# Gated recurrence with the second half of its tokens in reversed order: one level product for chunk j and chunk j+4, three merged key buffers

## What is computed

```python
qf = silu(q) * DK ** -0.5
logf = minimum(log_sigmoid(z) + log1p(lb * exp(-z)), 0)   # z = clip(f, -30, 30)
kf = -expm1(logf)
# per head, over tokens t:  state = exp(logf_t) * state + outer(kf_t, v_t);  o_t = qf_t @ state
# in chunks: o = (qf * exp(bcum)) @ state_before
#              + sum over j <= i of (qf_i . exp(bcum_i - bcum_j) . kf_j) v_j
o = rmsnorm(o, norm_g) * silu(g)
```

## Time and profile before

| | us |
|---|---|
| median of 3 runs (lowest, highest) | 2679.35 (2674.05, 2681.57) |
| the profiled execution, its own time | 2681.49 |
| its span from first to last instruction | 2679.7 |
| PE busy | 2566.4 (96%) |
| DVE busy | 1528.2 (57%) |
| POOL busy | 1217.8 (45%) |
| ACT busy | 575.9 (21%) |
| PE products of L470 (896 records), busy | 104.7 |
| mean granted TensorE clock, share of full | 0.984 |

### The profile page before, as it was taken

The page is one execution under the profiler, slowest core; times in us unless marked ns, Lnnn a source line. Parts: engine busy times, 40 slices in busy tenths (PEclk is TensorE's granted clock), DMA queues, the critical chain, the costliest instruction groups (busy, mean ns, idle before and its releaser), DMA issues.

```text
span 2679.7 us, 32172 instructions
## 1 busy us (share of the span) xinstructions
PE 2566.4 (96%) x11898; PEld 2120.0 (79%) x11898; DVE 1528.2 (57%) x1639; ACT 575.9 (21%) x737; POOL 1217.8 (45%) x941
## 2 busy tenths in 40 slices
PE   8999999899999999999899999977989999999997
PEld 5788877788888888888778787766878888888885
DVE  6794666677777773976675747544572222531223
ACT  3110344322222222111121214233331100121000
POOL 0433332222222222333577677711766666766663
PEclk9999999999999999999999999989999999999998
DMA  6322111111111111433644344321433223432323
GB/s 227 118 71 90 63 59 63 55 38 42 39 39 39 39 47 69 151 118 110 237 167 161 126 141 158 129 83 43 154 114 98 94 95 101 151 101 94 102 95 110
DMA packets 84882, 269.87 MB, mean 101 GB/s; under 512 B 7888, under 2 KB 9296, under 8 KB 83792
## 3 DMA queue, kind: packets, MB, share of 16 engines
q1 hardware_dynamic: 71760, 243.80, 27.2%
q10 hardware_dynamic: 13056, 25.17, 2.7%
HBM read 224.37 MB, written 44.56 MB: 100 GB/s over the span
## 4 chain that ended last, share of the span: by engine, by line
PE 77%; DVE 12%; issue 4%; ACT 4%; DMA 2%; POOL 1%; DVEq 0%; SPq 0%; ACTq 0%; POOLq 0%
PE ps L349 22%; PE ps L350 22%; PE ps L351 22%; PE xb L470 4%; DVE macc L701 1%; DVE lxc L904 1%; PE ps L397 1%; POOL w_lo L1813 1%; DVE lgx L704 1%; DVE lga L926 1%; DMA w_kv<-wall 1%; DVE cdev L707 1%; DVE xb L837 1%; DVE xa L837 1%; DVE yb_lo L689 1%
## 5 line engine op out<-in xcount | busy, mean ns | idle before, releaser
L1813 POOL TENSOR_TENSOR w_lo<-w_raw,w_hi 128x1024 fp32r<-128x1024 f32 x312 | 789.9, 2532 | 26.1
L1810 POOL TENSOR_TENSOR small<-small 128x1 f32<-128x1 f32 x312 | 85.6, 274 | 1407.2 <-PE ps L351 1209.1
L349 PE MATMUL ps<-h_hi,w_hi 128*128 128x512 f32 x1408 | 558.4, 397 | 9.8 <-DVE hg_zc L1030 8.0
L351 PE MATMUL ps<-h_hi,w_lo 128*128 128x512 f32 x1408 | 550.1, 391 | 0.0
L350 PE MATMUL ps<-h_lo,w_hi 128*128 128x512 f32 x1408 | 549.6, 390 | 0.0
L349 PE MATMUL ps<-yb_hi,w_hi 128*128 128x512 f32 x1024 | 405.6, 396 | 25.7 <-DVE yb_lo L689 13.5
L350 PE MATMUL ps<-yb_lo,w_hi 128*128 128x512 f32 x1024 | 401.4, 392 | 0.0
L351 PE MATMUL ps<-yb_hi,w_lo 128*128 128x512 f32 x1024 | 401.3, 392 | 0.0
L1811 POOL TENSOR_SCALAR w_hi<-w_raw 128x1024 fp32r<-128x1024 f32 x312 | 354.5, 1136 | 0.0
L349 PEld LDWEIGHTS ps<-h_hi,w_hi 128*128 128x128 f32 x1408 | 265.3, 188 | 66.2 <-issue 12.9
L351 PEld LDWEIGHTS ps<-h_hi,w_lo 128*128 128x128 f32 x1408 | 265.1, 188 | 56.6
(11 more groups left out here) (262 smaller groups left out, 2965.1 us busy)
## 6 DMA issues: line engine op xcount, KB each, us to landing
w_raw<-wall SPq DMA_DIRECT2D x312, 512.0 KB, 3.5
gst<-gate_d SPq DMA_DIRECT2D x24, 512.0 KB, 4.3
w_kv<-wall SPq DMA_DIRECT2D x16, 512.0 KB, 4.0
x_d<-xx ACTq DMA_DIRECT2D x16, 512.0 KB, 3.0
gate_d<-sigb SPq DMA_DIRECT2D x12, 512.0 KB, 2.6
gate_d<-gbuf SPq DMA_DIRECT2D x12, 512.0 KB, 2.8
xs_xa<-x_d ACTq DMA_DIRECT2D x12, 512.0 KB, 5.1
x_sb<-xT SPq DMA_DIRECT2D x2, 2048.0 KB, 15.1
```

What stands on the lines that cost most here:

```text
L349: nc.tensor.matmul(out, wh, xh, start=start, stop=False)
L351: return nc.tensor.matmul(out, wl, xh, start=False, stop=stop)
L1810: nc.gpsimd.tensor_tensor(small[:, 13:14], small[:, 12:13], small[:, 12:13], ALU.add)
L1813: nc.gpsimd.tensor_tensor(w_lo[:, u], w_raw[:, u], w_hi[:, u].bitcast(F32), ALU.subtract).then_inc(w_split, 1)
```

## The change

Tokens 512 to 1023 are held in reversed order for the whole recurrence of a head: the clip, the query and the value copy are done as two instructions of 512 columns, the second of which reads PSUM backwards, and the two copies of the output do the same. In a reversed chunk the earlier block of a pair is the right one, so the keys of chunk j use the left blocks and those of chunk j+4 the right blocks of one 128-column key operand: `hkp`, three buffers of 512 columns, all of whose columns are now written. A level is then 4 products of 128 keys by 2 x 64 queries instead of 8 of 128 by 64. Level 1 needs merged keys too (a new `tensor_scalar` per head). The order of chunks in time is 0, 1, 2, 3, 7, 6, 5, 4. DVE's wait in the loop of levels is for level l-2. The mask differs between the halves, is uint8 with 512 columns per level, is loaded in the first head ahead of the load of `ub`, and needs no cast. The memsets of the key buffers go.

```diff
 LEVELS = 7
+TIME_ORDER = (0, 1, 2, 3, 7, 6, 5, 4)
...
         ones = at("ones", 512, [P, P])
-        lvmask = at("lvmask", 1024, [P, LEVELS, CHUNK // 2], U8)
...
         gbuf = at("gbuf", CONV + 2 * UB + 4 * ROW, [P, T])
+        lvmask = at("lvmask", CONV + 2 * UB + 3 * ROW, [P, LEVELS, HALF], U8)
...
         assert origin + TOP <= nc.sbuf_usable_end, (origin + TOP, nc.sbuf_usable_end)
-        names = ("zc", "sp", "sn", "f", "b", "k", "q", "qp2", "kp0", "kp1", "vt", "vtok", "gg", "attn",
+        names = ("zc", "sp", "sn", "f", "b", "k", "q", "qp2", "kp", "kp2", "vt", "vtok", "gg", "attn",
...
+        hkp = [at(f"hg_kp{i}", ARENA + (8 + i // 2) * ROW + i % 2 * HROW, [P, HALF]) for i in range(3)]
...
         out_stored = sem("out_stored")
+        def pairs(x, at0, step, n, skip, c, one=1):
+            x = x[:]
+            return bass.AP(x.tensor, x.offset + at0, [x.ap[0], [step, 2], [skip, n], [one, c]])
+        def turned(x, n):
+            return x[:, 0:HALF] if n == 0 else x[:, HALF:T][:, ::-1]
...
+            def in_order(n, product):
+                for i in range(n):
+                    c = TIME_ORDER[i]
+                    mm = product(slice(i * CHUNK, (i + 1) * CHUNK), slice(c * CHUNK, (c + 1) * CHUNK))
+                return mm
...
                 pe.wait_ge(lv_free, (LEVELS + 1) * h + max(l - 1, 1))
-                keys = hg["k"] if l == 1 else hg[f"kp{l % 2}"]
-                for c in range(NCH):
+                for c in range(NCH // 2):
                     w = CHUNK // 2
-                    at0 = (l % 2) * HALF + c * w
-                    mm = nc.tensor.matmul(xb[:, at0:at0 + w], keys[:, c * CHUNK:(c + 1) * CHUNK],
-                                          hqp[l % 4][:, c * w:(c + 1) * w], start=True, stop=True)
+                    mm = nc.tensor.matmul(pairs(xb, (l % 2) * HALF + c * w, HALF // 2, 1, w, w)[:, :, 0],
+                                          hkp[l % 3][:, c * CHUNK:(c + 1) * CHUNK],
+                                          pairs(hqp[l % 4], c * w, HALF // 2, 1, w, w)[:, :, 0], start=True, stop=True)
...
-                per_chunk(NCH - 1, lambda c, ch: nc.tensor.transpose(xa[:, ch], hg["kr"][:, ch], ident[:])).then_inc(ktr_done, 1)
+                in_order(NCH - 1, lambda slot, ch: nc.tensor.transpose(xa[:, slot], hg["kr"][:, ch], ident[:])).then_inc(ktr_done, 1)
...
-                per_chunk(NCH - 1, lambda c, ch: nc.tensor.matmul(
-                    xa[:, ch], hg["krt"][:, ch], hg["vtok"][:, ch], start=True, stop=True)).then_inc(ds_done, 1)
+                in_order(NCH - 1, lambda slot, ch: nc.tensor.matmul(
+                    xa[:, slot], hg["krt"][:, slot], hg["vtok"][:, ch], start=True, stop=True)).then_inc(ds_done, 1)
...
-                def product(c, ch):
-                    mm = nc.tensor.matmul(xb[:, ch], hg["vtok"][:, ch], hg["attn"][:, ch], start=True, stop=c == 0)
-                    if c:
-                        before = slice((c - 1) * CHUNK, c * CHUNK)
+                def product(slot, ch):
+                    mm = nc.tensor.matmul(xb[:, ch], hg["vtok"][:, ch], hg["attn"][:, ch], start=True, stop=slot.start == 0)
+                    if slot.start:
+                        before = slice(slot.start - CHUNK, slot.start)
...
-                per_chunk(NCH, product).then_inc(out_done, 1)
+                in_order(NCH, product).then_inc(out_done, 1)
...
                 sub(TM, par[:, :, HLB], par[:, :, HLB]).then_inc(consts_ready, 1)
-                dve.wait_ge(mask_in, 16)
-                v.tensor_copy(lvmask[:], mask_f[:])
...
             s.end(KB // 2)
-            def sides(t, c):
-                both = t[:].rearrange("p (n two c) -> p n two c", two=2, c=c)
-                return both[:, :, 0], both[:, :, 1]
-            def all_blocks(x, c):
-                return x.to_broadcast([P, HALF // c, c])
+            def left(x, c):
+                return pairs(x, 0, HALF + c, HALF // 2 // c, 2 * c, c)
+            def right(x, c):
+                return pairs(x, c, HALF - c, HALF // 2 // c, 2 * c, c)
+            def left_end(x, c):
+                return pairs(x, c - 1, HALF + 1, HALF // 2 // c, 2 * c, c, 0)
+            def right_end(x, c):
+                return pairs(x, 2 * c - 1, HALF + 1 - 2 * c, HALF // 2 // c, 2 * c, c, 0)
+            def packed(x, c):
+                return pairs(x, 0, HALF // 2, HALF // 2 // c, c, c)
+            def merged(x, c):
+                return pairs(x, 0, c, HALF // 2 // c, 2 * c, c)
...
                 if l > 1:
-                    mul(sides(hg[f"kp{l % 2}"], c)[0], sides(k, c)[0], sides(b, c)[0])
-                mul(hqp[l % 4][:].rearrange("p (n c) -> p n c", c=c), sides(q, c)[1], sides(f, c)[1]).then_inc(lv_ready, 1)
+                    mul(merged(hkp[l % 3], c), left(k, c), left(b, c))
+                mul(packed(hqp[l % 4], c), right(q, c), right(f, c)).then_inc(lv_ready, 1)
...
-                bl, _ = sides(b, c)
-                fl, fr = sides(f, c)
...
-                    done(v.tensor_copy(bl, fr))
+                    done(v.tensor_copy(left(b, c), right(f, c)))
                 else:
-                    done(mul(bl, bl, all_blocks(fr[:, :, c - 1:c], c)))
-                return s.at(mul(fr, fr, all_blocks(fl[:, :, c - 1:c], c)))
+                    done(mul(left(b, c), left(b, c), right_end(f, c)))
+                return s.at(mul(right(f, c), right(f, c), left_end(f, c)))
...
                 v.memset(small[:, 14:15], 0.0)
-                chunks = hg["attn"][:].rearrange("p (ch n two c) -> p ch n two c", ch=NCH, two=2, c=c)
-                mask = lvmask[:, l - 1].rearrange("p (o n c) -> p o n c", o=1, c=c).to_broadcast([P, NCH, CHUNK // 2 // c, c])
-                bank = xb[:, (l % 2) * HALF:(l % 2 + 1) * HALF].rearrange("p (ch n c) -> p ch n c", ch=NCH, c=c)
-                v.copy_predicated(chunks[:, :, :, 1], mask, bank).then_inc(lv_free, 1)
+                bank = xb[:, (l % 2) * HALF:(l % 2 + 1) * HALF]
+                v.copy_predicated(right(hg["attn"], c), packed(lvmask[:, l - 1], c), packed(bank, c)).then_inc(lv_free, 1)
...
                     ch = slice(c * CHUNK, (c + 1) * CHUNK)
+                    end = TIME_ORDER[c] * CHUNK + (CHUNK - 1 if c < NCH // 2 else 0)
                     ins = v.scalar_tensor_tensor(hg["state"][:, ch], hg["state"][:, (c - 1) * CHUNK:c * CHUNK],
-                                                 f[:, (c + 1) * CHUNK - 1:(c + 1) * CHUNK], xa[:, ch], ALU.mult, ALU.add)
+                                                 f[:, end:end + 1], xa[:, ch], ALU.mult, ALU.add)
...
                 dve.wait_ge(mm_done, 2 * m + 1)
-                v.tensor_scalar(zc[:], ps[0][:], CLIP, -CLIP, ALU.min, ALU.max).then_inc(evac[0], 1)
+                for n in range(2):
+                    ins = v.tensor_scalar(zc[:, n * HALF:(n + 1) * HALF], turned(ps[0], n), CLIP, -CLIP, ALU.min, ALU.max)
+                ins.then_inc(evac[0], 1)
                 if first(h):
-                    for t in ("b", "kp0", "kp1"):
-                        last = s.at(v.memset(hg[t][:], 1.0))
-                    s.wait(last)
+                    dve.wait_ge(mask_in, 16)
+                    s.wait(s.at(v.memset(b[:], 1.0)))
...
                 s.at(v.tensor_scalar(k[:], sn[:], lb1, 0.0, ALU.mult, ALU.max))
-                last = s.at(v.memset(sides(b, 1)[1], 1.0))
+                s.at(v.tensor_scalar(merged(hkp[1], 1), left(sn, 1), lb1, 0.0, ALU.mult, ALU.max))
+                last = s.at(v.memset(right(b, 1), 1.0))
...
-                v.scalar_tensor_tensor(q[:], ps[1][:], DK_SCALE, hg["qs"][:], ALU.mult, ALU.mult).then_inc(evac[1], 1)
+                for n in range(2):
+                    ins = v.scalar_tensor_tensor(q[:, n * HALF:(n + 1) * HALF], turned(ps[1], n), DK_SCALE, turned(hg["qs"], n),
+                                                 ALU.mult, ALU.mult)
+                ins.then_inc(evac[1], 1)
...
                     if l > 2:
-                        dve.wait_ge(lv_done, LEVELS * h + l - 1)
+                        dve.wait_ge(lv_done, LEVELS * h + l - 2)
...
                 act.wait_ge(out_done, h)
-                a.activation(hg["osq"][:], xb[:], ACT.Square).then_inc(osq_done, 1)
-                copy(hg["oc"][:], xb[:]).then_inc(oc_done, 1)
+                for n in range(2):
+                    ins = a.activation(hg["osq"][:, n * HALF:(n + 1) * HALF], turned(xb, n), ACT.Square)
+                ins.then_inc(osq_done, 1)
+                for n in range(2):
+                    ins = copy(hg["oc"][:, n * HALF:(n + 1) * HALF], turned(xb, n))
+                ins.then_inc(oc_done, 1)
...
                 act.wait_ge(mm_done, 2 * m + 3)
-                copy(hg["vt"][:], ps[0][:]).then_inc(evac[0], 1)
+                for n in range(2):
+                    ins = copy(hg["vt"][:, n * HALF:(n + 1) * HALF], turned(ps[0], n))
+                ins.then_inc(evac[0], 1)
...
```

(10 more changed lines are left out.)

## The result

The changed kernel takes 2645.12 us in the median of 4 runs (2642.02 to 2650.51), beside 2677.32 for the kernel before (2674.05 to 2681.57, 4 runs): 32 us less. The ratio is 0.9881 with a 95% interval of 0.9858 to 0.9904, that is 26 to 38 us less.

A forecast was written before the change was run, and what follows sets the result against it. PE's own issue list was taken as the bound, with DVE the feeder to fear. -48.8 + 4.0 + 1.5 + 0.7 - 0.3 = -42.9 us gave 2636.4 us, likeliest 2629 to 2642, 8 in 10 from 2629 to 2655.

The forecast's parts named there:

- the first rival: DVE bounds the heads: 27 half-tile instructions each 0.06 us longer from three-level patterns, +13 us, 2649; chance 0.26.
- the signs: Trace marks of a right forecast: 448 records, two levels in 1.75 us, diagonals 5.6 closer, `kr` wait 0.3 to 0.8.
- Level products, -48.8: PE's levels in the heads: 448 records fewer at 0.109 us each, -48.8 us, or 6.1 per head.
- DVE up to kr, +4.0: DVE from diagonal to `kr`: PE waits 0.5 us per head at the key transposes, +4.0 us (bounds 0 and 12).
- The third key buffer: DVE's loop of levels: the buffer was to take away its waits of 0.72 and 2.57 us.
- Instructions with three-level patterns: DVE's masks and patterns in two pieces at L704 and L971: no change taken.
- The second: Rival: new patterns put DVE's 22 two-operand products at half rate, +61 us, 2742; with mild forms, chance 0.04.
- the third: Rival: PE's level time goes by columns, so nothing is gained there and the first head adds 1.9, 2681; chance 0.04.
- the fourth: Rival: DVE keeps up everywhere and the mask costs its issue only, 2631; counted within the forecast's 0.66.
- First head, +1.5 and +0.7: First head: mask load ahead of `ub` delays the clip, +1.5 us; DVE's clip, key instruction and query, +0.7.
- Start, -0.3: Kernel start: the mask leaves the queue ahead of a load for which PE waited 0.32 us, -0.3 us.
- Hidden splits: Steady heads: split clip (+0.08 us), new key instruction and ACT's splits lie under other waits; with those gone, 0.8.

The follow-up runs named there:

- the second measurement: The changed kernel run again with no edit: 2644.22 us (6 runs) against 2679.57 for the kernel before, ratio 0.9884; it also gave a second profile.
- the run with halves: The changed kernel with each level product made twice with 64 columns, same merged keys: 2680.72 us (10 runs), ratio 1.0014 to the kernel before.
- the gate edit: The changed kernel with DVE's output gate moved from ahead of `kr` to behind it: 2637.04 us (5 runs), ratio 0.9853 to the kernel before.

## Why the prediction was right, and where it was off

The measured time lies in the range of 8 in 10, and the direction is right, but the gain was forecast at 42.9 us and came as 32 (35 in the second measurement), outside the range that I called likeliest (2629 to 2642). It lies in the band that I gave to the first rival, 2642 to 2668, whose mechanism isn't there, so that the time falls in the range owes something to the range being drawn wide for another reason. Of the signs, the number of records and the price of a level came; the diagonals are 3.9 or 5.1 us closer and not 5.6, PE waits for `kr` by 0.8 to 1.2 and not 0.3 to 0.8, and it also waits at level 4, which no sign named.

- *Level products, -48.8.* Right, slightly more: 56 levels by (1.745 - 0.85) = 50.1. That a record is paid and not its columns is shown by the run with halves. The Trainium skill's rule for matmuls by themselves, that the gap grows with the columns (TensorE: Matmul & The Clock Gate, Back-to-back issue gap), would have given no gain. These products don't follow it: 0.109 us a record at 64 columns, 0.106 at 128.
- *DVE up to kr, +4.0.* This step failed. The waits came to 7.5 + 4.1 = 11.6 us, and with 0.2 us for each of the 12, shown by the gate edit's periods, to 14. Two errors. First, I held DVE's chain against PE at one place, the key transposes. PE's `level` has two waits, one for its operands and one for its bank, and I held neither against DVE at level 4. The bank is free once the copy out of level 2 is done; that copy is issued behind the level's operands on DVE, and POOL's first pass falls on them. Second, `kr` was late by 0.8 to 1.2, not 0.5: the wait for level 1 was 0.7, not 0.5; the second pass stretched two instructions by 0.9 and 2.1, 3.0 in all, where I took 1.8 and 0.6 to 1.1 more; and the first pass cost 0.9 and 2.2 in the four heads that wait at level 4, where I went by the one head with 2.06. Five of the eight heads of the kernel before had lost 2.9 to 3.1 to it already, behind the room that DVE had then.
- *The third key buffer.* I let it take two waits of DVE away. They went with the shorter levels; without the buffer nothing changes (run with the wait back).
- *Instructions with three-level patterns.* No change taken, none came: products 0.69, copies 1.31 and 0.70 where POOL is idle. The first rival gave about the right size (PE waiting 1 to 2 us per head) by a mechanism that isn't there. The second falls by the same rows, the third by the run with halves, the fourth because `kr` is late in every head and the mask costs 1.24 us and not 0.47.
- *First head, +1.5 and +0.7.* Measured +1.24 and +0.66, the latter +0.44 in the second profile. The 0.2 between them is PE and not DVE: its granted clock from the clip to the diagonal was 0.64 of full in the first profile, where its half tile ended too late for a wait to be seen, and 0.80 in the second, where it waited 0.90 for the query. The key instruction takes 0.48.
- *Start, -0.3.* The wait of 0.32 is gone, and from the first of those 112 products to the next group on PE 27.51 us pass in all eight profiles without the load at the start, 28.10 and 27.90 in the two with it: -0.4 to -0.6. The rest of what the start gained in that execution was not tried.
- *Hidden splits.* The clip is two instructions in 1.28 against 1.23 for one. The fixed cost of 0.125 us that the Trainium skill gives (VectorE: DVE Perf Modes, section on the TRN2 errata) is not reached.

With measured sizes the sum is -50.1 + 14 + 1.2 + 0.7 - 0.5 = -34.7, inside the interval of -26 to -38.

## What to carry to other kernels

When the bounding engine's list gets shorter, every wait in that list has to be held against its feeder again, bank and buffer waits as well as operands, and not only the last one of the chain. A float32 product with few columns costs its record (here 0.11 us with 64 columns as with 128): pack what shares a stationary operand. An edit that is worth nothing in the kernel before (the gate behind `kr`) can be worth 7 us in the changed one, so the order on a feeder is worth another look after the change.

## What was not expected of the hardware

POOL's passes stretch DVE's products of two SBUF operands (0.69 to 2.88 us; such a product ends about 0.55 us after the pass), but not a predicated copy out of PSUM that runs beside them (1.32 against 1.30), so what a pass costs depends on what it meets: 3.1, 2.2, 1.9 or 1.6 us of DVE for the first pass in the same kernel. The Trainium skill, GPSIMD Engine Reference, section Specifications, says that GpSimd shares its SBUF interfaces with VectorE, with contention where a DVE instruction has two SBUF inputs or a two-port mode; the trace agrees for two SBUF inputs. And 0.16 us in the start of POOL's pass behind one load (10.70 or 10.86 after the diagonal) decided between heads of 61.2 and 62.4 us, which makes the sum over the heads differ between executions of the same kernel, 432.4 to 435.7 here over four profiles: two of the changed kernel, the one with DVE's wait back and the one with the mask behind `ub`, edits that showed no wait of their own in these heads.
